# A hybrid attention step on one core: the output projection in 512-column matmuls, by token groups

## The reference

```python
h = rmsnorm(x, norm_g) @ w_in                  # 2048 -> 5648: q, k, v, gates of both branches
oa = sliding-window attention of qa, ka, va     # 16 heads of 64, chunks of 64, sinks
og = gated linear attention of qg, kg, vg, la   # 4 heads, key 128, value 256
mix = concat(oa * silu(ga), rmsnorm(og) * silu(gg))
y = x + mix @ w_out                             # w_out 2048 x 2048
```

## Time and profile before

| what | us |
|---|---|
| median of 3 runs | 2030.36 (2029.29 to 2030.73) |
| the profiled execution, its span | 2029.8 |
| TensorE matmul busy | 1937.9 (95%) |
| VectorE busy | 835.3 (41%) |
| GpSimd busy | 640.0 (32%) |
| ScalarE busy | 447.5 (22%) |

### The profile page before, as it was taken

One profiled execution on the slowest core, in us unless ns is written; L12 is line 12 of the kernel. 1 busy time (PEld: TensorE's weight loads), 2 busy tenths in 40 slices (PEclk: granted clock), 3 DMA queues, 4 the chain that ended last, 5 costly groups with the idle time before them and its releaser, 6 DMA issues.

```text
span 2029.8 us, 33101 instructions
## 1 busy us (share of the span) xinstructions
PE 1937.9 (95%) x12160; PEld 1809.8 (89%) x12160; DVE 835.3 (41%) x1553; ACT 447.5 (22%) x1064; POOL 640.0 (32%) x509
## 2 busy tenths in 40 slices
PE   5999999989999999999999999999999899999999
PEld 4899999867777779999988888889999899999999
DVE  6454453134334331111277777875555640000000
ACT  6211111133333331000244344441001120000000
POOL 1433333111112222233334434332323333333331
PEclk8999999989999999999999999999999999999999
DMA  6322222222222322221322222333433472222221
GB/s 214 128 65 65 65 65 75 78 69 75 71 68 75 96 64 88 71 71 56 92 76 84 75 83 75 86 96 120 143 110 107 142 233 88 88 86 81 86 88 34
DMA packets 237665, 184.43 MB, mean 91 GB/s; under 512 B 15345, under 2 KB 236017, under 8 KB 236178
## 3 DMA queue, kind: packets, MB, share of 16 engines
q1 hardware_dynamic: 159618, 131.99, 21.3%
q10 hardware_dynamic: 78000, 51.81, 9.1%
HBM read 133.27 MB, written 52.31 MB: 91 GB/s over the span
## 4 chain that ended last, share of the span: by engine, by line
PE 77%; DVE 13%; issue 4%; ACT 3%; DMA 2%; ACTq 1%; DVEq 0%; POOL 0%; SPq 0%; POOLq 0%
PE p L1557 14%; PE p L1559 14%; PE p L1558 14%; PE p L1631 7%; PE p L1632 7%; PE p L1633 7%; DVE xn L1723 4%; PE p L504 2%; PE p L487 2%; ACT work L551 2%; PE p L713 2%; PE p L497 2%; DVE work L627 1%; DVE work L613 1%; PE p L724 1%
## 5 line engine op out<-in xcount | busy, mean ns | idle before, releaser
L1557 PE MATMUL p<-x_hi,w_lo 128*128 128x384 f32 x2112 | 730.9, 346 | 0.0
L1559 PE MATMUL p<-x_hi,w_hi 128*128 128x384 f32 x2112 | 708.5, 335 | 0.0
L1558 PE MATMUL p<-x_lo,w_hi 128*128 128x384 f32 x2112 | 708.2, 335 | 0.0
L450 POOL TENSOR_TENSOR w_hi<-raw,small 128x512 fp32r<-128x512 f32 x176 | 186.3, 1059 | 870.9 <-PE p L1559 859.6
L1557 PEld LDWEIGHTS p<-x_hi,w_lo 128*128 128x128 f32 x2112 | 398.2, 189 | 41.6 <-issue 39.2
L1558 PEld LDWEIGHTS p<-x_lo,w_hi 128*128 128x128 f32 x2112 | 398.4, 189 | 0.4
L1559 PEld LDWEIGHTS p<-x_hi,w_hi 128*128 128x128 f32 x2112 | 397.8, 188 | 0.0
L1631 PE MATMUL p<-w_hi,x_lo 128*128 128x256 f32 x1152 | 328.2, 285 | 5.7 <-DVE x_lo L1796 5.7
L1632 PE MATMUL p<-w_lo,x_hi 128*128 128x256 f32 x1152 | 327.9, 285 | 0.0
L1633 PE MATMUL p<-w_hi,x_hi 128*128 128x256 f32 x1152 | 327.7, 284 | 0.0
L455 POOL TENSOR_TENSOR w_lo<-raw,w_hi 128x512 fp32r<-128x512 f32 x176 | 228.6, 1299 | 13.8
(11 more groups left out here) (181 smaller groups left out, 1842.7 us busy)
## 6 DMA issues: line engine op xcount, KB each, us to landing
raw<-in_w_in SPq DMA_DIRECT2D x176, 256.0 KB, 3.7
h_t<-xn SPq DMA_DIRECT2D x132, 192.0 KB, 1.9
raw<-in_w_out SPq DMA_DIRECT2D x32, 512.0 KB, 3.6
work<-h_t ACTq DMA_DIRECT2D x42, 256.0 KB, 5.2
out<-work ACTq DMA_DIRECT2D x76, 128.0 KB, 2.9
work<-h_t SPq DMA_DIRECT2D x24, 384.0 KB, 4.1
work<-h_t ACTq DMA_DIRECT2D x17, 512.0 KB, 5.6
work<-in_x_prompt SPq DMA_DIRECT2D x64, 128.0 KB, 3.5
```

Source lines behind the costliest of these rows:

```text
L450: pool.tensor_tensor(w_hi[:, k:k + 4, 0:n], w_raw(k, n), zeros[:, :].unsqueeze(1) .to_broadcast([P, 4, n]), ALU.add).then_inc(s_whi, 1)
L1557: pe.matmul(out, w_lo[:, k, :], x_hi[:, k, tok], start=(k == 0), stop=False)
L1558: pe.matmul(out, w_hi[:, k, :], x_lo[:, k, tok], start=False, stop=False)
L1559: mm = pe.matmul(out, w_hi[:, k, :], x_hi[:, k, tok], start=False, stop=(k == KT - 1))
```

## The change

The output stage alone is rewritten.

- A weight chunk is 512 columns (`WCH`), so there are four; the token groups n (three tiles of 128) are outermost. A group g is one n and one chunk: 12 groups, g // 4 is n. w_out is so loaded and split three times, once for each n.
- A slice is one k of 128 x 512. Raw, high and low weights have four slots each. SyncE loads slice u when the low half of u - 4 is done (`t_wlo`). ScalarE makes the high half (`high_w`), VectorE the low half (`low_w`). GpSimd does nothing in this stage.
- TensorE goes over four blocks b of four k; in each over the three tiles t; in each over the four k. Slots are released in the last tile (`t_wfree`, one count for each k). Three accumulators, one bank each; groups alternate between two sets of banks.
- The pieces are ordered by n first. Those of n = 0 come ahead of the stage; those of n + 1 are loaded and split in the second group of n (g = 1 and 5), one behind each slice k = 4 to 11 (`piece_after`).
- VectorE adds the tiles of group g - 1 behind `low_w(g, 2)`. SyncE issues the stores of y, and the residual loads behind them, at k = 6.

```diff
-WCH = 256
+WCH = 512
 NCH = D_MODEL // WCH
+NGRP = NG * NCH
...
-            return [(q, n, i) for q in range(4) for n in range(NG) for i in range(2)]
+            return [(q, n, i) for n in range(NG) for q in range(4) for i in range(2)]
...
+        def piece_after(g, k):
+            if g % NCH == 1 and g // NCH + 1 < NG and 4 <= k < 12:
+                return 8 * (g // NCH + 1) + k - 4
+            return None
...
+                def load_w_out(g, k):
+                    u = 16 * g + k
+                    if u >= 4:
+                        sp.wait_ge(t_wlo, u - 3)
+                    sp.dma_start(o_raw[k % 4], o_w[:, k, (g % NCH) * WCH:(g % NCH) * WCH + WCH])\
+                      .then_inc(t_w[k % 4], 16)
+                def store_y(g, t):
+                    sp.wait_ge(t_y, 6 + NG * g + t + 1)
+                    sp.dma_start(rows_of(y_p, y_s, NG * (g // NCH) + t, g % NCH), y_sb[:, t, :])\
+                      .then_inc(t_st[t], 16)
...
+                for k in range(4):
+                    load_w_out(0, k)
+                for t in range(NG):
+                    load_x_res(0, t)
+                load_pieces(4, 7)
                 store_last(0)
                 store_last(1)
+                load_pieces(7, 8)
...
+                for g in range(NGRP):
+                    for k in range(4 if g == 0 else 0, KT):
+                        load_w_out(g, k)
+                        if g == 0 and k == 5:
+                            store_last(2)
+                        if g > 0 and k == 6:
+                            for t in range(NG):
+                                store_y(g - 1, t)
+                                load_x_res(g, t)
+                        if piece_after(g, k) is not None:
+                            load_pieces(piece_after(g, k), piece_after(g, k) + 1)
...
+            def high_w(g, k):
+                u = 16 * g + k
+                act.wait_ge(t_w[k % 4], 16 * (u // 4) + 16)
+                if u < 4:
+                    act.wait_ge(s_wfree, 4 * N_ITEMS + (k + 5))
+                else:
+                    act.wait_ge(t_wfree, u - 3)
+                act.activation(o_hi[k % 4], o_raw[k % 4], ACT.Copy).then_inc(t_whi, 1)
...
+            high(0, 7)
+            for k in range(4):
+                high_w(0, k)
+            high(7, 8)
             item_silu(N_ITEMS, 2)
             decode.end()
+            for g in range(NGRP):
+                for k in range(4 if g == 0 else 0, KT):
+                    high_w(g, k)
+                    if piece_after(g, k) is not None:
+                        high(piece_after(g, k), piece_after(g, k) + 1)
...
+            def out_chunk(n, g, parity):
+                for b in range(4):
+                    for t in range(NG):
+                        if b == 0:
+                            pe.wait_ge(t_y, NG * g + (t + 1))
+                        out = banks[(3 + 3 * parity + t) % 8][:, 0:WCH]
+                        tok = slice(n * TN + t * P, n * TN + t * P + P)
                         for i in range(4):
+                            k = 4 * b + i
+                            if t == 0:
+                                pe.wait_ge(t_wlo, 16 * g + (k + 1))
+                                if k % 2 == 0:
+                                    pe.wait_ge(t_mlo, SLOTS + 8 * n + k // 2 + 1)
+                            pe.matmul(out, x_lo[:, k, tok], o_hi[i], start=(k == 0), stop=False)
+                            pe.matmul(out, x_hi[:, k, tok], o_lo[i], start=False, stop=False)
+                            mm = pe.matmul(out, x_hi[:, k, tok], o_hi[i], start=False, stop=(k == KT - 1))
+                            if t == NG - 1:
+                                mm.then_inc(t_wfree, 1)
+                        if b == 3 and t < NG - 1:
                             mm.then_inc(t_acc, 1)
...
+            def low_w(g, k):
+                dve.wait_ge(t_whi, 16 * g + k + 1)
+                if g == 0 and k < 4:
+                    dve.wait_ge(s_wfree, 4 * N_ITEMS + (k + 5))
+                dve.tensor_tensor(o_lo[k % 4], o_raw[k % 4], o_hi[k % 4].bitcast(F32), ALU.subtract)\
+                   .then_inc(t_wlo, 1)
...
+            low(0, 7)
+            for k in range(4):
+                low_w(0, k)
+            low(7, 8)
+            silu_g(N_ITEMS, 2)
+            for g in range(NGRP):
+                for k in range(4 if g == 0 else 0, KT):
+                    low_w(g, k)
+                    if g > 0 and k == 2:
+                        for t in range(NG):
+                            add(g - 1, t)
+                    if piece_after(g, k) is not None:
+                        low(piece_after(g, k), piece_after(g, k) + 1)
+            for t in range(NG):
+                add(NGRP - 1, t)
```

More of the change, by code:

```diff
@@ L241, in project @@
         t_mlo = sem("t_mlo")
-        t_w = [sem(f"t_w{i}") for i in range(2)]
+        t_w = [sem(f"t_w{i}") for i in range(4)]
         t_whi = sem("t_whi")
-        t_wready = sem("t_wready")
+        t_wlo = sem("t_wlo")
         t_wfree = sem("t_wfree")
-        t_x = [sem(f"t_x{i}") for i in range(NT)]
+        t_x = [sem(f"t_x{i}") for i in range(NG)]
         t_acc = sem("t_acc")
@@ L255, in pieces @@
         def pieces():
[L257 removed]
+            return [(q, n, i) for n in range(NG) for q in range(4) for i in range(2)]
         o_w = w_out.rearrange("(k p) n -> p k n", p=P)
[L260 to L262 removed]
+        o_raw = [raw[:, s * WCH:s * WCH + WCH] for s in range(4)]
+        o_hi = [w_hi[:, 4 * s:4 * s + 4, :].rearrange("p a n -> p (a n)") for s in range(4)]
+        o_lo = [w_lo[:, 4 * s:4 * s + 4, :].rearrange("p a n -> p (a n)") for s in range(4)]
         piece_sb = work[:, 0:3072].rearrange("p (s k n) -> p s k n", s=SLOTS, k=2)
         o_dec = work[:, 3072:4096].rearrange("p (k n) -> p k n", n=P)
[L265 to L266 removed]
+        x_res = work[:, 4096:5632].rearrange("p (t n) -> p t n", n=WCH)
+        y_sb = work[:, 5632:7168].rearrange("p (t n) -> p t n", n=WCH)
         def rows_of(p, s, t, c):
             if t < NTP:
[L270 to L271 removed]
+                return p[t * P:t * P + P, c * WCH:c * WCH + WCH]
+            return s[:, c * WCH:c * WCH + WCH]
         def is_gated_late(q, n):
             return q >= 2 and n == NG - 1
+        def piece_after(g, k):
+            if g % NCH == 1 and g // NCH + 1 < NG and 4 <= k < 12:
+                return 8 * (g // NCH + 1) + k - 4
+            return None
         w_v = w_in.rearrange("(k p) n -> p k n", p=P)
@@ L367, in out_loads @@
                 sp.wait_ge(s_wready, 4 * (N_ITEMS + 1))
-                load_w_out(0, 0)
-                load_w_out(0, 1)
+                for k in range(4):
[3 more added lines that the diff above has]
+                load_pieces(4, 7)
                 store_last(0)
                 store_last(1)
-                load_pieces(4, 6)
+                load_pieces(7, 8)
                 sp.dma_start(o_dec, o_t[D_MODEL // 2:D_MODEL, SEQ:TOK].rearrange("(k p) n -> p k n", p=P))\
                   .then_inc(t_dec, 16)
[L375 to L388, removed]
+                for g in range(NGRP):
[10 more added lines that the diff above has]
+                for t in range(NG):
+                    store_y(NGRP - 1, t)
+                for t in range(NG):
+                    sp.wait_ge(t_st[t], 16 * NGRP)
             def store_item(j, row, n_rows, gates=None):
@@ L1394, in _ @@
                 split(pool, j)
[L1396 to L1409, removed]
         @block.scalar
@@ L1614, in _ @@
             pe.wait_ge(sl_og, 4 * NT + 1)
[L1615 to L1624, removed]
-                        for i in range(4):
[L1626 to L1637, removed]
@@ L1638, in _ @@
                             mm.then_inc(t_acc, 1)
+            for n in range(NG):
+                with pe.Fori(0, NCH // 2) as c:
+                    out_chunk(n, 2 * c + NCH * n, 0)
+                    out_chunk(n, 2 * c + (NCH * n + 1), 1)
         @block.vector
@@ L1809, in _ @@
-            dve.sem_inc(t_y, NT)
-            low(0, 6)
-            silu_g(N_ITEMS, 2)
[L1812 to L1817, removed]
+            def low_w(g, k):
[4 more added lines that the diff above has]
+                   .then_inc(t_wlo, 1)
@@ new lines, in add @@
+            def add(g, t):
+                if t == NG - 1:
+                    dve.wait_ge(t_wfree, 16 * g + KT)
+                else:
+                    dve.wait_ge(t_acc, (NG - 1) * g + (t + 1))
+                dve.wait_ge(t_x[t], 16 * g + 16)
+                if g > 0:
+                    dve.wait_ge(t_st[t], 16 * g)
+                dve.tensor_tensor(y_sb[:, t, :], banks[(3 + 3 * (g % 2) + t) % 8][:, 0:WCH],
+                                  x_res[:, t, :], ALU.add).then_inc(t_y, 1)
@@ new lines, in _ @@
+            dve.sem_inc(t_y, 2 * NG)
+            low(0, 7)
+            for k in range(4):
+                low_w(0, k)
+            low(7, 8)
+            silu_g(N_ITEMS, 2)
+            for g in range(NGRP):
```

(7 more changed lines are left out.)

27 lines of the change are left out of this document (2 added, 25 removed).

## The result

The changed kernel takes 2046.98 us (median of 4 runs, 2045.4 to 2049.28), the kernel before in the same comparison 2029.82 us: a ratio of 1.0087, 95% interval 1.0072 to 1.0101. It is slower by 17 us, where 25 were forecast (2055, range 2035 to 2069). The profiled execution took 2049.28 us, its span is 2047.5.

The account below looks back on a forecast made before the run. The prediction took TensorE, busy 95% of the span, as the bound. From 1601.9 us its terms summed to 452.7 us against 427.9 before, 24.8 more, so a median of 2055 us, range 2035 to 2069.

Parts of the forecast that it names:

- idleness at the start: Start of the output stage: TensorE idles 5.9 us from 1601.9 while VectorE splits the first pieces ahead of the first slice.
- 1728 matmuls: Output stage: 512-column matmuls at 227 ns each take 392.3 us, a gain of 22.1.
- lower clock at the start: Start of the output stage: TensorE begins at the lower clock after its idleness, costing 2.5 us.
- gap in the second block: Early output stage: the late gate's store delays the loads of slices 6 and 7, a gap of 1.1 us.
- eleven add gaps: Group boundaries: VectorE's three adds delay slice 3, a gap of 1.75 plus 0.1 us each, 20.4 us in all.
- pieces: Second and sixth group: splitting pieces on VectorE starves TensorE, 15.8 us with restarts.
- transfers: Output stage loads and stores: taken to cost nothing, bounds 0 and 4 us.
- lower clock later: Behind the boundary gaps and starved blocks: TensorE at the lower clock, 11 us in all.
- tail: End of the stage: 3.0 us as before, plus a longer last add and a larger store, 3.7 us.
- fixed 13 ns: Each matmul: a fixed part beside its columns, read from the 256- and 384-column rows, giving 227 ns for 512 columns.
- three in eight of 11 gaps: 4 times, 7 us: Group boundaries: the lower clock follows four gaps, at the linear attention's rate, costing 7 us (0 to 19).
- rival B: Output stage: VectorE's order costs TensorE nothing, as adds and pieces fit; 2008 us, chance 0.12.

Follow-up runs that it names:

- all_moved: The changed kernel with pieces behind each block's last slice over two groups, adds behind slice 3, stores and residual loads behind slice 7's load: 2006.10 us.
- all_moved_256: all_moved with each 512-column matmul issued as two of 256 columns on the same data: 2027.86 us.
- pieces_back: all_moved with the pieces back where the changed kernel has them, one behind each slice of two blocks in the second and sixth group: 2021.19 us.
- all_moved_start: all_moved with only four pieces and the late gate's work moved around the first slices, other pieces behind slices 7 and 11, last gate stored later: 1996.24 us.
- both_moved: The changed kernel with the adds behind slice 3 and the pieces behind each block's last slice over two groups: 2041.56 us.
- adds_behind_3: The changed kernel with the three adds of the group before placed behind slice 3 instead of slice 2, nothing else: 2057.38 us.
- pieces_at_ends: The changed kernel with the sixteen pieces of token groups 1 and 2 each behind a block's last slice, over two groups: 2025.37 us.
- pieces_burst: The changed kernel with pieces behind each block's last slice and SyncE's stores and residual loads behind slice 7's load; adds stay behind slice 2: 2021.69 us.

## Why the prediction was right, and where its sizes were off

By its own terms, in the profiled execution of the changed kernel:

| term | forecast | measured |
|---|---|---|
| idleness at the start | 5.9 | 6.7 (1603.2 to 1609.84) |
| 1728 matmuls | 392.3 | 392.3 (227.0 ns) |
| lower clock at the start | 2.5 | 2.8 (12 starts at 427 ns for 227, two in between) |
| gap in the second block | 1.1 | 0.8 |
| eleven add gaps | 20.4 | 16.1 (1.46 each) |
| pieces | 15.8 | 17.1 (VectorE's order some 13, loads some 4) |
| transfers | 0 | 0.8 (one gap in the fifth group) |
| lower clock later | 11 | 4.0 (17 starts at 427 ns, three in between) |
| tail | 3.7 | 3.5 |

The pieces' 17.1 are the second group's 40.55 us less 34.15, and the sixth group's 48.83 less 34.15 and less the 4.0 of clock. The gap in the fifth group stands ahead of slice 7: ScalarE waited 1.07 us for its load there. The measured terms make 444.1 of the 444.3.

**Right:** the fixed 13 ns (all_moved against all_moved_256), and with it the gain of 22 us; the adds ahead of slice 3 (1.19 us gaps, eleven of them); the starvation by the pieces, in its larger part (pieces_back: 14.5 us by its two groups, 15.1 by the medians); the start (all_moved_start). The page "TensorE: Matmul & The Clock Gate" of the Trainium skill, Part 1 and Back-to-back issue gap, gives 215.7 ns for 512 columns. The traces disagree: they have 226.6 and 227.0.

**Off in size:** the sum was 8.4 us too high. Two terms were 11.3 too high, and the others together 2.9 too low, so that a part of the errors cancelled. The gap of an add boundary was put at 1.85 and is 1.46: VectorE's three adds take 1.79 from the first's start to the next subtraction, where the forecast took 2.1, and its hand-off to TensorE is 0.06 for 0.13. And "three in eight of 11 gaps: 4 times, 7 us" measured nothing: behind none of the eleven gaps did the clock fall (1.00 over 1840 to 2040). The rate was read from idleness of 2.0 to 2.1 us and laid on gaps that turned out to be 1.2. In both_moved, with gaps of 1.3 to 2.3, the lower level follows four of eleven. Its windows of 8 us around those four, and around four of the others:

```profile
1724.00:1732.00 8.00, 6.51 (x22) 5.21 (x23) 0.69 (x1) 1.08 (x2) 0.00 (x0) 0.79 0.23 81
1796.00:1804.00 8.00, 7.13 (x24) 5.70 (x25) 2.01 (x3) 1.91 (x4) 0.00 (x0) 0.79 0.43 136
1902.00:1910.00 8.00, 6.49 (x21) 5.22 (x22) 0.69 (x1) 1.04 (x2) 0.00 (x0) 0.79 0.23 80
1973.00:1981.00 8.00, 6.78 (x23) 5.46 (x24) 0.69 (x1) 0.86 (x2) 0.00 (x0) 0.79 0.19 66
1760.00:1768.00 8.00, 6.20 (x28) 5.12 (x28) 1.72 (x3) 2.22 (x4) 0.00 (x0) 1.00 0.29 100
1831.00:1839.00 8.00, 6.35 (x28) 4.93 (x28) 2.76 (x5) 2.74 (x4) 0.00 (x0) 1.00 0.57 193
1655.00:1663.00 8.00, 6.98 (x31) 5.77 (x32) 3.48 (x5) 3.43 (x6) 0.00 (x0) 1.00 0.41 131
1867.00:1875.00 8.00, 6.72 (x29) 5.55 (x30) 2.23 (x4) 2.56 (x5) 0.00 (x0) 1.00 0.18 62
```

The third number from the end is the clock: 0.79 behind gaps of 1.9, 2.1, 2.25 and 1.9, but 1.00 behind 1.8, 1.65, 2.2 and 2.2. So the size of the gap does not decide alone; of the six gaps of 1.9 us and more, four were followed by the lower level. Three in eight was of the right order for gaps of 2 us, and was laid on gaps of another size.

**Wrong, and in part hidden by luck:** the transfers. "I take nothing, bounds 0 and 4" stands against 0.8 us in the fifth group and some 4 for the pieces' loads in the second and sixth, where the forecast had set 13 us of transfers against some 13 until slice 7 is wanted. The number was hidden in the pieces' term, whose VectorE part, some 13, was forecast nearly 3 too high. The other reason, that behind the stores "stand only residuals and slice 7, which waits for slice 3 anyway", holds only as long as slice 3 is late. Its consequence, that without the adds' and pieces' wait on VectorE the gain would be there (rival B: 2008), is false for these two edits: both_moved has 2041.56, and adds_behind_3, with the adds alone, 2057. The load of slice 7 then stands behind the burst for 3.5 to 4.3 us, a wait that the forecast had not counted. Only together with SyncE's order does 2008 come out nearly as stated: all_moved has 2006.

## What to carry to other kernels

A wider matmul gains a fixed part for each one saved, and it can be read from two sizes already in the trace; what it costs is in how the operands' slots come free. Count the window between the release of a slot and its next use, and put nothing into an in-order queue ahead of the work of that window, neither adds on the vector engine nor stores ahead of a load. When a wait is taken away and the time rises, look for the queue that the wait had been covering: here moving the adds alone lost 10 to 16 us, and moving them together with the stores gained 19 (pieces_at_ends against all_moved). A part of such a loss can be the clock behind the new gaps: here about half of it.

## What the runs showed of the hardware that was not expected

- TensorE's clock did not fall behind any gap of 1.2 us: in pieces_burst eleven stand between 1640 and 2017, and the clock is 1.00 (its window):

```profile
1640.00:2017.00 377.00, 363.90 (x1592) 297.29 (x1591) 156.53 (x231) 123.37 (x192) 0.00 (x0) 1.00 0.54 183
```

  Behind gaps of about 2 us it fell in some cases to the lower level, and behind the start's 6 to 7 us in every kernel with the late start.
- The kernel's own first stage is not constant: the last projection matmul started anywhere from 1597.1 to 1603.4 us in the same code, more than several of the effects looked for. Whether the stage from that point on repeats better is not shown: each kernel was profiled once.
- VectorE's subtraction of 128x768, beside GpSimd's splits, took 2.2 us in the mean of six (13.05 us) at the start of the stage before, up to 3.16; in the changed kernel, with GpSimd idle there, all 24 take 0.95 to 0.96. That GpSimd's splits are the cause was not tested by a run of its own.
